# Delta stage of a hybrid encoder: the second and third sweep of the block solve on the open corner only

## Chip, cores and metric

One NeuronCore of one Trainium2 chip. The metric is the device time of the whole kernel in microseconds, as the median of a set of runs.

## The reference, cut to what matters

Two encoder layers over 2048 tokens of width 1024, in float32. Each layer projects its input, feeds one part to a gated DeltaNet branch (4 heads of width 128, run forward and backward over the sequence) and another to an attention branch, and maps both back. A final norm closes the trunk. The change lies in the DeltaNet branch, which for one direction is this, per chunk of tokens:

```python
lower = where(strict, einsum('bnhid,bnhjd->bnhij', k_beta, kc) * decay, 0.0)
a_mat = lower + eye(C)
rhs = concatenate([vc * bc, k_beta * exp(gc)[..., None]], axis=-1)
sol = triangular_solve(a_mat, rhs, left_side=True, lower=True, unit_diagonal=True)
u, w = sol[..., :Dv], sol[..., Dv:]
attn = einsum('bnhid,bnhjd->bnhij', qc, kc) * decay

def step(state, inp):                       # scan over the chunks
    v_new = u_i - w_i @ state
    o_i = (q_i * exp(g_i)[..., None]) @ state + a_i @ v_new
    state = state * exp(g_last)[..., None] + k_dec.T @ v_new
```

What has to be computed per chunk is thus the inverse of a unit triangular matrix, applied to the values, and a state that is carried from chunk to chunk.

## The kernel before, in words

The kernel is a sequence of stages per layer: input projection, token tables, `delta_net`, attention, output projection; and `finish` once. Each stage is one block in which the five engines run programs of their own, in a fixed order written by hand, and meet through semaphores. Only `delta_net` is touched.

**Tiling.** Its chunks are 128 tokens, not 64, so there are `NC` = 16 of them. "Side" 0 walks them forward, side 1 backward, so a step handles two chunks, and in each the 4 heads. A tile of one side is 128 partitions x 4 heads x 128 columns, one bank of PSUM wide. `each(out, left, right)` (L1146) issues the 4 matmuls of a tile, one per head; every one of them is recorded at line 1148, and shows as two records in the trace, since it is a float32 matmul.

**The inverse.** The 128x128 triangular matrix of a chunk is cut into 4x4 blocks of `BLK` = 32. The inverses of the 32x32 diagonal blocks come from a lane-wise elimination (`eliminate`, L1382 on GpSimd, L1465 on VectorE), in 5 groups of chunks, many blocks at once. `prepare_lanes` and `scale_lanes` on VectorE (L1478, L1486) bring a group in and out; the results go through DRAM and come back as block-diagonal tiles `dd` and `dt` (`load_dd`, `load_dt`). The rest of the inverse comes from a block substitution: `off_diagonal` (TensorE, L1184) and `masked_blocks` (VectorE, L1502) make `btc`, the strictly block-triangular factor; then three sweeps, each `y = dd - btc.T @ y` with `y = dd` at first: `substitute` (TensorE, L1190) and `update` (VectorE, L1507). Sweep k makes the blocks right that lie k off the diagonal. All three sweeps work on the whole 128x128 tile.

**The order.** The item of step j+1 (its inverse) is made during step j, between the pieces of the recurrence. TensorE's order in a step, each for both sides: `known`, `carried`, `off_diagonal`, `solve`, `turn_k`, from step 9 `turn_output`, `substitute` 1, `output`, `substitute` 2, `state_step`, `substitute` 3. The item of step 0 is made ahead of the loop, the last step makes none. VectorE's order in a step: from step 9 `mean_squares`; `remainder`, from step 9 `inverse_root`, `masked_blocks`, from step 9 `gate`, `update` 1, `visit`, `update` 2, `new_state`, `update` 3; then in steps 1 and 4 `prepare_lanes(3)` and `(4)`, in steps 2, 5 and 7 `scale_lanes(2)`, `(3)` and `(4)`. `scale_lanes(g)` waits for all of the elimination of group g.

GpSimd eliminates group 1 ahead of the loop and then has, in steps 0 to 7, a share of the columns of groups 2 to 4 (`SCAN_COLS`), each followed by `masked_scores` of the next step (L1394), which `output` of that step needs. From step 8 on it joins the two visits of a chunk, squares them and multiplies by the inverse mean instead. ScalarE scales what comes out of PSUM. SyncE issues all loads and stores of the stage in one order; `load_dd(j + 2)` waits for the third `update` of both sides of item j+1.

Of the kernel before, what the change touches and what calls it, by code (L numbers as in the profile page):

```python
# [7 lines left out]
P = 128  # L8
F32 = mybir.dt.float32
F32R = mybir.dt.float32r  # L10
ALU = mybir.AluOpType
# [23 lines left out]
BLK = 32  # L35
# [839 lines left out]
HEADS = range(DN_HEADS)  # L875
# [67 lines left out]
def delta_net(nc, a, c, l):  # L943
# [6 lines left out]
    with ExitStack() as stack, semaphores(nc, names) as s:  # L950
# [8 lines left out]
        dd, dt = (c.sq_acc[:, n * SEQ // 2:(n + 1) * SEQ // 2].rearrange("p (n h t) -> p n h t", n=N_DIR, t=P)  # L959
                  for n in range(2))  # L960
# [6 lines left out]
        r, se, oa, sq, ot, z, o, first_o, btc, y, am, kk = (room[:, n] for n in range(12))  # L967
# [6 lines left out]
        bank = lambda n: ps[:, n, :].rearrange("p (h t) -> p h t", h=DN_HEADS)  # L974
        mask = lambda side, kind: masks[:, side, kind, :].unsqueeze(1).broadcast_to([P, DN_HEADS, P])
        heads = lambda side: range(side * DN_HEADS, (side + 1) * DN_HEADS)
        inverse, chain, outer, turned = (lambda side: bank(side)), (lambda side: bank(2 + side)), \
            (lambda side: bank(4 + side)), (lambda side: bank(6 + side))

        with nc.Block() as block:  # L980
# [164 lines left out]
            def _(pe):  # L1145
                def each(out, left, right):  # L1146
                    for h in HEADS:
                        mm = nc.tensor.matmul(out[:, h, :], left[:, h, :], right[:, h, :], start=True, stop=True)  # L1148
                    return mm
# [40 lines left out]
                def substitute(side, i, k):  # L1190
                    if k == 1:
                        pe.wait_ge(s["dd_loaded"], 64 * (i + 1))
                        pe.wait_ge(s[f"btc{side}"], i + 1)
                        each(inverse(side), btc[:, side], dd[:, side]).then_inc(s[f"p{side}"], 1)
                    else:
                        pe.wait_ge(s[f"y{side}"], 3 * i + k - 1)
                        each(inverse(side), btc[:, side], y[:, side]).then_inc(s[f"p{side}"], 1)

                def known(side, j):
                    pe.wait_ge(s[f"state{side}"], j + 1)  # L1200
# [44 lines left out]
                for k in (1, 2, 3):  # L1245
                    for side in SIDES:
                        substitute(side, 0, k)
                for j in range(NC):
                    more = j + 1 < NC
                    for side in SIDES:  # L1250
                        known(side, j)
                    for side in SIDES:
                        carried(side, j)
                    for side in SIDES:
                        if more:
                            off_diagonal(side, j + 1)
                    for side in SIDES:
                        solve(side, j)
                    for side in SIDES:
                        if more:  # L1260
                            turn_k(side, j + 1)
                    if j > FIRST_VISITS:
                        for side in SIDES:
                            turn_output(side, j - 1)
                    for side in SIDES:
                        if more:
                            substitute(side, j + 1, 1)
                    for side in SIDES:
                        output(side, j)
                    for side in SIDES:  # L1270
                        if more:
                            substitute(side, j + 1, 2)
                    for side in SIDES:
                        state_step(side, j)
                    for side in SIDES:
                        if more:
                            substitute(side, j + 1, 3)
# [177 lines left out]
            def _(dve):  # L1455
# [51 lines left out]
                def update(side, i, k):  # L1507
                    dve.wait_ge(s[f"p{side}"], 3 * i + k)
                    if k == 1:
                        dve.wait_ge(s["dd_loaded"], 64 * (i + 1))  # L1510
                        if i:
                            dve.wait_ge(s[f"solve{side}"], i)
                    nc.vector.tensor_tensor(y[:, side], dd[:, side], inverse(side), ALU.subtract).then_inc(s[f"y{side}"], 1)

                def visit(side, j):
                    dve.wait_ge(s[f"out{side}"], j + 1)
# [53 lines left out]
                for k in (1, 2, 3):  # L1570
                    for side in SIDES:
                        update(side, 0, k)
                    if k == 1:
                        prepare_lanes(2)
                scale_lanes(1)
                for j in range(NC):
# [14 lines left out]
                    if more:  # L1591
                        for side in SIDES:
                            update(side, j + 1, 1)
                    for side in SIDES:
                        visit(side, j)
                    if more:
                        for side in SIDES:
                            update(side, j + 1, 2)
# [605 lines left out]
def build(nc, a):  # L2204
# [6 lines left out]
    with ExitStack() as stack:  # L2211
# [23 lines left out]
        for l in range(DEPTH):  # L2235
            input_projection(nc, a, c, l)
            token_inputs(nc, a, c, l)
            delta_net(nc, a, c, l)
            with ExitStack() as inner:
                c.delta = inner.enter_context(nc.sbuf_tensor(f"ahead_delta{l}", [P, DN_HEADS, SEQ], F32))  # L2240
                c.gates = inner.enter_context(nc.sbuf_tensor(f"ahead_gates{l}", [P, DN_HEADS, SEQ], F32R))
                c.w_out = inner.enter_context(nc.sbuf_tensor(f"ahead_w{l}", [P, 2, KT * P], F32))
                attention(nc, a, c, l)
                output_projection(nc, a, c, l)
# [72 lines left out]
```

## Time and profile before

| | |
|---|---|
| runs | 4149.61, 4154.29, 4154.32 us; median 4154.29 |
| profiled execution | 4156.78 us, its span 4155.0 us |
| TensorE (PE) | 3827.0 us busy, 92% of the span |
| VectorE (DVE) | 2846.4 us, 69% |
| ScalarE (ACT) | 1874.4 us, 45% |
| GpSimd (POOL) | 715.7 us, 17% |
| granted TensorE clock, mean | 0.955 |

The busy shares are averages over stages that differ much. GpSimd's 17%, for instance, lies nearly all in two places of each layer. PEld is TensorE's weight load, which overlaps its matmuls; SPq is the queue of SyncE, at which DMAs are issued. In the rows, "x16" is the number of merged instructions, and for TensorE 128*64 would be a weight tile of 128 rows and 64 columns. A bracket at the end of a timeline row is the engine's idle time before it and who ended it. The dn_banks are PSUM; the dn_sb_room tile holds `y`, `btc`, `r`, `am` and eight more, c_sq_acc holds `dd` and `dt`. Matmul ends are modelled and pipelined, so the time between two starts says more than a duration.

### The profile page before, as it was taken

What the parts mean: (1) busy time and instruction counts of PE and PEld (TensorE: products, weight loads), DVE (VectorE), ACT (ScalarE), POOL (GpSimd) and SP (SyncE); (2) the same over time, 40 slices, a digit from 0 to 9 for tenths busy, and PEclk for the clock granted to TensorE, in tenths of its full rate; (3) what the DMA queues carried; (4) which work ended last, traced back from release to release, by engine and by line L of the source; (5) the groups of instructions that cost most, each with busy time, mean ns of one, the idle gap of its engine ahead of it and who ended that gap; (6) DMA issues with size and microseconds to landing.
All of it is one profiled execution on the core that took longest, in us unless ns stands there. A gap on an engine that the chain in (4) does not pass through costs nothing. (4 is left out here: it accounts for less than half of the span.)

```text
span 4155.0 us, 55812 instructions
## 1 busy us (share of the span) xinstructions
PE 3827.0 (92%) x19078; PEld 3004.4 (72%) x19078; DVE 2846.4 (69%) x3424; ACT 1874.4 (45%) x2552; POOL 715.7 (17%) x761
## 2 busy tenths in 40 slices
PE   7999996699799999999999999966997999999896
PEld 5877785599766776767778777845996767776674
DVE  5674182676689999975266723745776999999743
ACT  4222212255377777772132222133554777777511
POOL 0022102596400000000001211037942000000000
PEclk9999998899899999999999999978998999999997
DMA  2111174445530000005322113654454200000335
GB/s 117 72 66 73 64 257 133 125 135 153 142 121 22 25 24 22 25 13 176 144 103 77 62 72 128 221 148 117 136 153 128 93 26 24 22 25 20 90 145 227
DMA packets 335765, 407.71 MB, mean 98 GB/s; under 512 B 105872, under 2 KB 255504, under 8 KB 315224
## 3 DMA queue, kind: packets, MB, share of 16 engines
q1 hardware_dynamic: 332728, 384.67, 28.9%
q10 hardware_dynamic: 2880, 20.97, 1.2%
q8 instruction: 95, 1.56, 0.2%
q14 instruction: 62, 0.51, 0.0%
HBM read 265.70 MB, written 139.66 MB: 98 GB/s over the span
## 5 line engine op out<-in xcount | busy, mean ns | idle before, releaser
L1854 DVE TENSOR_REDUCE att_sb_part<-att_banks 128x1 f32<-128x512 f32 x992 | 680.4, 687 | 102.7 <-PE att_banks L1739 88.8
L1841 ACT ACTIVATE att_sb_probs<-att_banks 128x1024 f32<-128x1024 f32 x512 | 525.1, 1026 | 314.0 <-PE att_banks L1767 313.8
L1872 DVE TENSOR_TENSOR att_sb_p_lo<-att_sb_probs,att_sb_p_hi 128x1024 fp32r<-128x1024 f32 x512 | 622.8, 1216 | 22.3 <-ACT att_sb_p_hi L1845 22.2
L1845 ACT ACTIVATE att_sb_p_hi<-att_sb_probs 128x1024 fp32r<-128x1024 f32 x512 | 544.1, 1063 | 16.1
L341 PE MATMUL proj_banks<-proj_sb_h_hi,proj_sb_w_hi 128*128 128x512 f32 x1600 | 500.9, 394 | 9.8 <-DVE proj_sb_pad L535 9.8
L341 PE MATMUL proj_banks<-proj_sb_h_lo,proj_sb_w_hi 128*128 128x512 f32 x1600 | 498.7, 393 | 0.0
L341 PE MATMUL proj_banks<-proj_sb_h_hi,proj_sb_w_low 128*128 128x512 f32 x1600 | 497.6, 392 | 0.0
L1148 PE MATMUL dn_banks<-dn_sb_room 128*128 128x128 f32 x3072 | 379.6, 283 | 58.0 <-DMA dn_sb_room<-proj 21.3
L401 POOL TENSOR_TENSOR c_low_squares<-c_sq_acc,proj_sb_high_squares 128x2048 fp32r<-128x2048 f32 x28 | 141.0, 5037 | 1679.8 <-ACT c_sq_acc L462 1679.8
L1148 PEld LDWEIGHTS dn_banks<-dn_sb_room 128*128 128x128 f32 x3072 | 368.0, 198 | 80.6 <-DMA dn_sb_room<-proj 30.9
L1766 PE MATMUL att_banks<-att_sb_q,att_sb_k 128*128 128x512 f32 x1024 | 407.0, 397 | 3.2 <-DVE att_sb_q L1866 1.9
L1767 PE MATMUL att_banks<-att_sb_q,att_sb_k 68*128 68x512 f32 x1024 | 409.1, 400 | 0.0
L1784 PE MATMUL att_banks<-att_sb_p_hi,att_sb_v_hi 128*65 128x512 f32 x1024 | 403.1, 394 | 1.4 <-DVE att_sb_p_lo L1872 1.4
L1739 PE MATMUL att_banks<-att_sb_k,att_sb_q 128*128 128x512 f32 x992 | 399.4, 404 | 3.9 <-DVE att_sb_part L1854 3.9
L1784 PE MATMUL att_banks<-att_sb_p_lo,att_sb_v_hi 128*65 128x512 f32 x1024 | 402.8, 393 | 0.0
L1784 PE MATMUL att_banks<-att_sb_p_hi,att_sb_v_lo 128*65 128x512 f32 x1024 | 400.8, 391 | 0.0
L341 PEld LDWEIGHTS proj_banks<-proj_sb_h_hi,proj_sb_w_hi 128*128 128x128 f32 x1600 | 301.4, 189 | 84.7 <-issue 11.0
L341 PEld LDWEIGHTS proj_banks<-proj_sb_h_lo,proj_sb_w_hi 128*128 128x128 f32 x1600 | 301.0, 188 | 75.6
L341 PEld LDWEIGHTS proj_banks<-proj_sb_h_hi,proj_sb_w_low 128*128 128x128 f32 x1600 | 300.8, 188 | 72.4
L617 DVE SCALAR_TENSOR_TENSOR proj_sb_out<-proj_sb_pad,proj_sb_taps,proj_sb_out 128x2048 f32<-128x2048 f32 x96 | 276.6, 2882 | 3.4
L535 DVE TENSOR_TENSOR proj_sb_out<-proj_banks,proj_sb_scale 128x1024 f32<-128x1024 f32 x56 | 68.5, 1223 | 272.7 <-PE proj_banks L341 272.7
L1739 PEld LDWEIGHTS att_banks<-att_sb_k,att_sb_q 128*128 128x128 f32 x992 | 189.7, 191 | 80.0 <-DVE att_sb_part L1854 7.9
(233 smaller groups left out, 5412.0 us busy)
## 6 DMA issues: line engine op xcount, KB each, us to landing
proj<-proj_sb_out SPq DMA_DIRECT2D x40, 1024.0 KB, 3.9
dn_sb_kq<-proj SPq DMA_DIRECT2D x64, 512.0 KB, 4.7
proj_sb_w_raw<-in_w_in SPq DMA_DIRECT2D x52, 536.0 KB, 3.6
dn_sb_room<-proj SPq DMA_DIRECT2D x32, 768.0 KB, 5.1
att_sb_q<-att_q SPq DMA_DIRECT2D x64, 256.0 KB, 2.6
x_res<-ahead_delta SPq DMA_DIRECT2D x16, 1024.0 KB, 4.1
proj_sb_pad<-proj SPq DMA_DIRECT2D x24, 512.0 KB, 4.7
proj<-proj_sb_out ACTq DMA_DIRECT2D x12, 1024.0 KB, 4.3
```

Source lines behind the costliest of these rows:

```text
L341: mm = nc.tensor.matmul(ps[:, 2 * half + n, :], w[:, u, k, :], h[:, k, at:at + QB], start=(k == 0 and w is w_hi and h is h_hi), stop=(k == ...
L401: nc.gpsimd.tensor_tensor(low, raw, high[:].bitcast(F32), ALU.subtract).then_inc(s["squares_split"], 1)
L617: nc.vector.scalar_tensor_tensor(out=out[:, u, :], in0=src, scalar=taps[:, u, j:j + 1], in1=out[:, u, :], op0=ALU.mult, op1=ALU.add).then_ ...
L1148: mm = nc.tensor.matmul(out[:, h, :], left[:, h, :], right[:, h, :], start=True, stop=True)
L1739: nc.tensor.matmul(ps[:, 4 + u % 2, :], q1[:, slot, tile * P:(tile + 1) * P], k1[:, slot % 2, keys * QB:(keys + 1) * QB], start=True, stop ...
L1766: nc.tensor.matmul(out, k1[:, slot % 2, keys], q1[:, slot, :], start=True, stop=False)
L1767: mm = nc.tensor.matmul(out, k2[:, slot % 2, keys], q2[:, slot, :], start=False, stop=True)
L1784: mm = nc.tensor.matmul(ps[0:DH + 1, 6 + kv, :], part_v[:, kv, tile, 0:DH + 1], part_p[:, at, m, :], start=opens, stop=(tile == NC - 1 and ...
L1841: nc.scalar.activation(probs[:, pair % 2], ps[:, 2 * (pair % 2):2 * (pair % 2) + 2, :], ACT.Exp, scale=SCALE).then_inc(s["exp_done"], 1)
L1845: nc.scalar.activation(p_hi[:, pair % SLOTS], probs[:, pair % 2], ACT.Copy).then_inc(s["hi_done"], 1)
L1854: nc.vector.tensor_reduce(part[:, w // NQ, w % NQ:w % NQ + 1], ps[:, 4 + w % 2, :], AX.X, ALU.max) \
L1872: nc.vector.tensor_tensor(p_lo[:, pair % SLOTS], probs[:, pair % 2], p_hi[:, pair % SLOTS].bitcast(F32), ALU.subtract).then_inc(s["lo_done ...
```

## The change

`open_rows` and `open_cols` name the corner of a side that is still open in sweep k: for side 0 the first 128 - 32 k rows and the last 128 - 32 k columns, for side 1 the mirror of it. In the second and the third sweep both engines work on that corner alone, 64x64 and 32x32: the matmul takes those weight columns of `btc` (they are the rows of the result) and those columns of `y`, with all 128 partitions in the sum as before, and the subtraction takes those rows and columns. The first sweep, the waits, the order and the numbers of instructions stay.

```diff
+        open_rows = lambda side, k: slice(0, P - k * BLK) if side == 0 else slice(k * BLK, P)
+        open_cols = lambda side, k: slice(k * BLK, P) if side == 0 else slice(0, P - k * BLK)
@@ substitute (TensorE), k = 2, 3
                         pe.wait_ge(s[f"y{side}"], 3 * i + k - 1)
-                        each(inverse(side), btc[:, side], y[:, side]).then_inc(s[f"p{side}"], 1)
+                        rows, cols = open_rows(side, k), open_cols(side, k)
+                        for h in HEADS:
+                            mm = nc.tensor.matmul(inverse(side)[rows, h, cols], btc[:, side, h, rows], y[:, side, h, cols],
+                                                  start=True, stop=True)
+                        mm.then_inc(s[f"p{side}"], 1)
@@ update (VectorE)
-                    nc.vector.tensor_tensor(y[:, side], dd[:, side], inverse(side), ALU.subtract).then_inc(s[f"y{side}"], 1)
+                        nc.vector.tensor_tensor(y[:, side], dd[:, side], inverse(side), ALU.subtract).then_inc(s[f"y{side}"], 1)
+                    else:
+                        rows, cols = open_rows(side, k), open_cols(side, k)
+                        nc.vector.tensor_tensor(y[rows, side, :, cols], dd[rows, side, :, cols], inverse(side)[rows, :, cols],
+                                                ALU.subtract).then_inc(s[f"y{side}"], 1)
```

## Rows read from the trace of the kernel before

**Rows 1.** Stretches: bounds, length; busy PE, PEld, DVE, ACT, POOL; clock, DMA.

```profile
825.00:970.00 145.00, 139.34 (x1219) 138.13 (x1218) 101.45 (x170) 76.52 (x259) 130.63 (x208) 0.99 0.46 133
...
976.40:981.00 4.60, 4.60 (x21) 4.60 (x22) 2.16 (x6) 2.12 (x9) 0.00 (x0) 0.50 0.20 48
...
981.00:1108.00 127.00, 126.59 (x1127) 125.81 (x1126) 93.43 (x189) 64.66 (x234) 64.03 (x57) 1.00 0.53 145
```

**Rows 2.** Timeline of a late step: start, us, engine, line, count, idle before; last row a group.

```profile
1001.23 7.31 PE L1148 MATMUL dn_banks<-dn_sb_room 128*128 128x128 f32 x64
...
1004.11 0.69 DVE L1513 TENSOR_TENSOR dn_sb_room<-c_sq_acc,dn_banks 128x512 f32<-128x512 f32 x1 [0.20 <-PE dn_banks L1148]
...
1006.79 0.69 DVE L1527 TENSOR_TENSOR dn_sb_state<-dn_sb_room,dn_banks 128x512 f32<-128x512 f32 x1 [0.21 <-PE dn_banks L1148]
...
1008.38 3.74 PE L1148 MATMUL dn_banks<-dn_sb_state,dn_sb_kq 128*128 128x128 f32 x32
...
1009.18 0.68 DVE L1534 TENSOR_REDUCE dn_sb_mean<-dn_sb_room 128x4 f32<-128x512 f32 x1
1009.33 1.80 SPq L1054 DMA_DIRECT2D c_sq_acc<-d_blk  x4
...
1010.87 2.15 DVE L1497 SCALAR_TENSOR_TENSOR dn_sb_room<-dn_banks,c_tok,dn_sb_vv 128x128 f32<-128x128 f32 x8
...
1013.74 1.95 PE L1148 MATMUL dn_banks<-dn_sb_room 128*128 128x128 f32 x16
...
1017.27 1.95 PE L1148 MATMUL dn_banks<-c_sq_acc,dn_sb_room 128*128 128x128 f32 x16
...
1019.05 7.31 PE L1148 MATMUL dn_banks<-dn_sb_room 128*128 128x128 f32 x64
...
L1148 PE MATMUL dn_banks<-dn_sb_room 128*128 128x128 f32 x3072 | 379.6, 283 | 58.0 <-DMA dn_sb_room<-proj 21.3 <-DVE dn_sb_room L1513 19.4 <-DVE dn_sb_room L1497 17.1
```

**Rows 3.** Timeline around the seam between steps 7 and 8; last, the second layer.

```profile
952.99 2.50 POOL L1397 TENSOR_TENSOR dn_sb_room<-dn_sb_att,dn_sb_masks 128x512 f32<-128x512 f32 x2
...
959.07 7.31 PE L1148 MATMUL dn_banks<-dn_sb_room 128*128 128x128 f32 x64
...
969.82 0.25 POOL L1392 TENSOR_TENSOR dn_sb_lane_inv<-dn_sb_lane_inv,dn_sb_lane_tmp 128x31 f32<-128x31 f32 x1
...
970.11 2.89 DVE L1488 TENSOR_TENSOR dn_sb_lane_mat<-dn_sb_lane_inv,dn_sb_lane_beta 64x1024 f32<-64x1024 f32 x1 [3.00 <-POOL dn_sb_lane_inv L1392]
...
976.38 3.78 PE L1148 MATMUL dn_banks<-dn_sb_room 128*128 128x128 f32 x16 [4.64 <-DVE dn_sb_room L1497]
...
3014.72 2.88 DVE L1488 TENSOR_TENSOR dn_sb_lane_mat<-dn_sb_lane_inv,dn_sb_lane_beta 64x1024 f32<-64x1024 f32 x1 [3.02 <-POOL dn_sb_lane_inv L1392]
```

**Rows 4.** Groups of weight loads by form: after the bar busy us and mean ns.

```profile
L1148 PEld LDWEIGHTS dn_banks<-dn_sb_room 128*128 128x128 f32 x3072 | 368.0, 198 | 80.6 <-DMA dn_sb_room<-proj 30.9 <-DVE dn_sb_room L1513 19.8 <-DVE dn_sb_room L1497 19.2
...
L1784 PEld LDWEIGHTS att_banks<-att_sb_p_hi,att_sb_v_hi 128*65 128x65 f32 x1024 | 140.8, 138 | 75.0 <-DVE att_sb_p_lo L1872 2.8 <-issue 0.4
...
L352 PEld LDWEIGHTS proj_banks<-c_low_squares,proj_sb_w_hi 128*32 128x32 f32 x112 | 12.1, 108 | 4.8
```

**Rows 5.** Timeline of TensorE in the input projection, with and without 128*32.

```profile
204.88 0.61 PE L341 MATMUL proj_banks<-proj_sb_h_hi,proj_sb_w_low 128*128 128x512 f32 x2
205.33 0.40 PE L352 MATMUL proj_banks<-proj_sb_high_squares,proj_sb_w_hi 128*32 128x512 f32 x1
205.57 0.62 PE L341 MATMUL proj_banks<-proj_sb_h_hi,proj_sb_w_hi 128*128 128x512 f32 x2
...
216.00 0.63 PE L341 MATMUL proj_banks<-proj_sb_h_lo,proj_sb_w_hi 128*128 128x512 f32 x2
216.47 0.63 PE L341 MATMUL proj_banks<-proj_sb_h_hi,proj_sb_w_low 128*128 128x512 f32 x2
```

**Rows 6.** Timeline of VectorE in the token tables: smaller operations out of PSUM.

```profile
673.88 0.42 DVE L809 TENSOR_TENSOR tab_sb_x<-tab_banks,tab_sb_low 128x256 f32<-128x256 f32 x1
...
675.09 0.29 DVE L818 COPY tab_sb_token_sums<-tab_banks 128x128 f32<-128x128 f32 x1
```

## The prediction

> **What bounds the kernel now.** I read the view of stretches first, cut at the seam that the timeline shows inside the delta stage of the first layer [rows 1]. From 825 to 970 us (steps j = 0 to 7) TensorE is busy 139.3 of 145 us, but GpSimd is busy 130.6 of 145 as well, in 208 instructions, and the list of waits has none of GpSimd's there: the rest of its time is the small gap behind each instruction of its dependent chain. From 981 to 1108 us (steps 8 to 15) TensorE has 126.6 of 127 us at the full clock and GpSimd only 64. So there are two regimes.
>
> The timeline of a late step [rows 2] shows what TensorE's line looks like: output, sweep 2, state and sweep 3 of both sides are one run of 64 records (two records to a matmul, eight matmuls for each of the four) from 1001.23 to the next group at 1008.38, which is 7.15/64 = 0.112 us from record to record. The same group starts again at 1019.05: a step is 17.82 us, with no gap in it.
>
> The seam [rows 3] is where the two regimes meet. GpSimd's last elimination instruction for lane group 4 ends at 970.07; only then can VectorE start `scale_lanes(4)`, for which it has waited 3.00 us; the `remainder` of step 8 stands behind it on VectorE, and TensorE, which needs that for `solve`, idles 4.64 us and starts at 976.38. The second layer has the same wait, 3.02 us at 3014.72. Since GpSimd waited for nobody on the way, the time of the seam is GpSimd's and not TensorE's.
>
> **The change, part by part.** *Fewer columns, TensorE.* Per item the second and the third sweep have 2 sides x 4 heads = 8 matmuls each, so 16 records each. At 0.112 us that is 1.79 us per sweep, 3.57 us per item. A record of the second sweep now loads 64 instead of 128 weight columns and streams 64 instead of 128; of the third, 32 and 32.
>
> No row shows such a record, so I bound the record-to-record time from both sides. The low end is proportional: 0.056 and 0.028 us. What speaks for it: a weight load's own duration falls with its columns, 198 ns at 128, 138 at 65, 108 at 32, about 0.9 ns a column over a constant near 80 ns that overlaps [rows 4]. The high end is 0.112 us, unchanged: the 128-column pace is the shortest that rows 2 to 6 have, and nothing in them shows that instructions can follow more closely. As the loads do shrink, I stay nearer to the low end, with some room for a fixed part: 0.062 us for the second and 0.045 us for the third. Gain per item: 16 x (0.112 - 0.062) + 16 x (0.112 - 0.045) = 0.80 + 1.07 = 1.87 us. Behind each sweep the first full load (state, then `known`) has only a short matmul to hide under instead of a long one: 0.05 us twice, taken off. Left are 1.77 us per item; proportional scaling would give 2.24 us, the unchanged pace 0.
>
> *Switching the array's shape.* The matmuls with 64 and 32 output rows stand between full ones. The nearest rows are in the input projection [rows 5]: two 128*128 matmuls, then one 128*32, then 128*128 again. The pair takes 0.45 us, the 128*32 one 0.24 us, three in 0.69; two neighbours without any switch take 0.47 us. So a switch costs less than 0.01 us there; I take 0. The upper bound is the full latency of a record being waited out, mean 0.283 against a pace of 0.112 [rows 2, 4]: 0.17 us per switch, four switches a step, 0.68 us. The Trainium skill, "TensorEngine Tiling (Array Packing)", section Key Properties, says that changing the tiling mode, as against the tile, drains TensorE; by that rule the sum would lose those 0.68 us a step and the kernel come out near 4139 us. Rows 5, where such a change happens twice in every three matmuls, don't show it.
>
> *VectorE.* Its two subtractions per side shrink from 128x512 (0.69 us) to 64x256 and 32x128. The nearest rows are a 128x256 subtraction at 0.42 us and a 128x128 copy at 0.29 us [rows 6]. That takes (0.27 + 0.40) x 2 = 1.3 us a step off an engine that isn't the bound; by itself worth nothing, and at worst (fixed costs, no shrinking) 0.
>
> *What is late next in steps 8 to 14.* In the times of rows 2, with sweep 2 at 0.5 us a side and sweep 3 at 0.36: output ends 1003.0, sweep 2 at 1004.0, state at 1005.8 (0.89 a side), sweep 3 at 1006.5; `known` starts there instead of at 1008.38. It needs the new state: VectorE starts 0.20 us behind the end of a side's state matmuls and takes 0.69 us [rows 2], so 1005.8 for side 0 (0.7 us to spare) and 1006.7 for side 1, needed at 1007.4. Sweep 3 needs the second update, which can't start before VectorE has done both visits (1003.9) and ends by 1004.8; it is needed at 1005.8. Further on, `remainder` started 2.5 us behind `known` (1010.87 against 1008.38) because two mean squares stood in front of it, from 1009.18; they now start 0.1 us sooner relative to `known`, so `solve` finds it with the same 0.7 us to spare (8 pieces from 1010.87 for 2.15 us, `solve` at 1013.74). The last update frees `dd` for SyncE's four loads, at 1009.33 before; issued by 1011.1, needed at 1017.27. No wait is added, and SyncE's order stays. So in these seven steps the whole 1.77 us comes through.
>
> *Steps 0 to 7 and the first item.* They get the same 1.77 us each, and none of it reaches the end. VectorE reaches `scale_lanes(4)` up to 14 us earlier and waits there until 970.1 as before. Already on the way TensorE meets GpSimd: `output` of step 7 starts at 959.07, and its masked scores come off GpSimd at 952.99 + 2.50 = 955.49 [rows 3], so from there only 3.6 us of lead fit. The sweeps of item 0 lie ahead of `scale_lanes(1)`, which waits for GpSimd too. Longer idling may lower TensorE's clock; it is at 0.50, the 1.2 GHz level, from 976.4 to 981.0 already [rows 1], behind the 4.64 us of idling, so I count no change.
>
> *Sum.* 7 steps x 1.77 us x 2 layers = 24.8 us. The profiled execution took 4156.8 us (span 4155.0): 4132.0. The median of the runs is 4154.3, 2.5 us lower, inside their spread of 4149.6 to 4154.3; taken from it the forecast is 4129.5, call it 4130 us.
>
> **Rivals.**
> *A: small matmuls have a large fixed cost*, by a drain at each switch or a floor near 0.08 us. By the floor: 32 x 0.032 x 14 = 14 us, 4140; by the drain: (1.77 - 0.68) x 14 = 15 us, 4139; both together: 4149. For it: no row has records closer than 0.112 us. Against it: rows 4 and 5.
> *B: GpSimd isn't a wall*, and all 32 items save: 4154 - 32 x 1.77 = 4098 us. For it: TensorE is 96% busy in steps 0 to 7. Against it: the waits of 3.00 and 3.02 us at the seam, equal in both layers.
> *C: the pace doesn't fall at all*, because instructions can't be issued faster: only VectorE's work shrinks, and that is covered. 4154 us.
> *D, slower:* the pace stays at 0.112 us and every switch drains. 0.68 us a step: 4.8 us in steps 8 to 14, and in steps 0 to 7 5.4 us, of which the seam absorbs 3.0. 7.2 us per layer, 4169 us. It decides once the four switches cost more than the records save, so from a fixed 0.44 us a switch at my pace, or from zero at an unchanged one. Rows 5 speak against it.
> That the change doesn't do what it says can be left out: sweep k only alters blocks k or more off the diagonal, and those are the rows and columns kept.
>
> **How the numbers follow.** Forecast 0.70 (its own range 4122 to 4137), A 0.13, B 0.07, C 0.05, D 0.05. A difference under 0.2%, 8.3 us, can't be told from no change. Faster by more than that (below 4146): the forecast, B and two thirds of A, 0.86. Within it: the rest of A and nearly all of C, 0.09. Slower: D, 0.05. The proportional end gives 14 x 2.24 = 31 us, 4123, and with the 2 or 3 us by which the medians of two sets differ 4120; that is the low end, with B left out. The high end takes in A but for its worst mixture: 4146.
>
> **What would show it.** In the stretch of steps 8 to 15 the distance from one `known` group to the next should fall from 17.82 to about 16.05 us, TensorE still without gaps; sweep 2 and 3 should stand as groups of about 1.0 and 0.7 us for 16 records. In steps 0 to 7 the step at the seam should still start its `solve` near 976.4 counted from the same start of the loop, with VectorE's wait for L1392 grown from 3.0 us to 5 or more. VectorE's subtractions should read about 0.42 and 0.29 us. I am wrong if the seam moves, if gaps on TensorE show up in steps 8 to 14, or if 16 small records take over 1.3 us.

## The result: 20 us, and where they lie

The changed kernel takes 4134.6 us in the median (4126.46 to 4140.22, five runs), the one before 4153.97 (4149.61 to 4154.32): a ratio of 0.995 (0.9937 to 0.9964). 4130 was forecast, 4120 to 4146 the range. The profiled execution is the slowest of the five, 4140.22 us with a span of 4138.4 and a mean clock of 0.951.

First the late step again, as [rows 2] have it. The columns are start, us, engine, line, count, idle before. Lines have moved by two to ten; L1201 is the new matmul of sweeps 2 and 3, L1522 its subtraction.

```profile
1007.56 3.84 PE L1150 MATMUL dn_banks<-dn_sb_state,dn_sb_kq 128*128 128x128 f32 x32
...
1009.10 0.86 DVE L1546 SCALAR_TENSOR_TENSOR dn_sb_mean<-dn_sb_mean,c_q_eps 128x4 f32<-128x4 f32 x1
...
1011.23 2.16 DVE L1503 SCALAR_TENSOR_TENSOR dn_sb_room<-dn_banks,c_tok,dn_sb_vv 128x128 f32<-128x128 f32 x8
1011.24 1.95 PE L1150 MATMUL dn_banks<-c_sq_acc,dn_sb_w 128*128 128x128 f32 x16
...
1018.34 1.95 PE L1150 MATMUL dn_banks<-dn_sb_room 128*128 128x128 f32 x16
1020.22 0.97 PE L1201 MATMUL dn_banks<-dn_sb_room 128*64 128x64 f32 x16
...
1020.94 0.87 DVE L1522 TENSOR_TENSOR dn_sb_room<-c_sq_acc,dn_banks 64x256 f32<-64x256 f32 x2
...
1021.12 2.05 PE L1150 MATMUL dn_banks<-dn_sb_room 128*128 128x128 f32 x16
1023.10 0.59 PE L1201 MATMUL dn_banks<-dn_sb_room 128*32 128x32 f32 x16
1023.62 3.84 PE L1150 MATMUL dn_banks<-dn_sb_state,dn_sb_kq 128*128 128x128 f32 x32
...
1023.81 0.59 DVE L1522 TENSOR_TENSOR dn_sb_room<-c_sq_acc,dn_banks 32x128 f32<-32x128 f32 x2
```

From `known` to `known` the step takes 1023.62 - 1007.56 = 16.06 us, against 17.82 before, still without a gap. Read by starts, sweep 2 takes 0.90 us (0.056 a record) and sweep 3 takes 0.52 us (0.033 a record). The full groups around them have grown: output takes 1.88 us and state 1.98, where a full group of 16 without a neighbour of another form takes 1.79. `known`, 3.57 us before, takes 3.68 (1007.56 to 1011.24). VectorE's subtractions come in pairs of 0.87 and 0.59 us, so about 0.44 and 0.30 each, close to the 0.42 and 0.29 that were put down.

Next the seam, and how the loop starts and ends. Its last three rows are of the second layer.

```profile
833.80 3.57 PE L1150 MATMUL dn_banks<-dn_sb_room 128*128 128x128 f32 x16 [4.18 <-DVE dn_sb_room L1503]
...
957.71 2.38 PE L1150 MATMUL dn_banks<-dn_sb_room 128*128 128x128 f32 x16 [1.52 <-POOL dn_sb_room L1403]
...
973.50 2.87 DVE L1494 TENSOR_TENSOR dn_sb_lane_mat<-dn_sb_lane_inv,dn_sb_lane_beta 64x1024 f32<-64x1024 f32 x1 [9.29 <-POOL dn_sb_lane_inv L1398]
...
979.75 3.78 PE L1150 MATMUL dn_banks<-dn_sb_room 128*128 128x128 f32 x16 [10.70 <-DVE dn_sb_room L1503]
...
1092.71 2.19 PE L1150 MATMUL dn_banks<-dn_sb_room 128*128 128x128 f32 x16 [1.01 <-DVE dn_sb_room L1503]
...
1105.63 2.11 PE L1230 MATMUL dn_banks<-c_ident,dn_sb_room 128*128 128x128 f32 x8 [5.15 <-POOL dn_sb_room L1421]
...
2867.14 3.78 PE L1150 MATMUL dn_banks<-dn_sb_room 128*128 128x128 f32 x16 [5.00 <-DVE dn_sb_room L1503]
...
3012.79 3.78 PE L1150 MATMUL dn_banks<-dn_sb_room 128*128 128x128 f32 x16 [9.88 <-DVE dn_sb_room L1503]
...
3139.29 2.12 PE L1230 MATMUL dn_banks<-c_ident,dn_sb_room 128*128 128x128 f32 x8 [5.14 <-POOL dn_sb_room L1421]
```

VectorE's wait for GpSimd has grown from 3.00 to 9.29 us and TensorE's gap from 4.64 to 10.70. Counted from `solve` of step 0, step 8 starts its `solve` after 145.95 us; before it was 145.39 (976.38 less 830.99 in the profile before). So eight narrower steps buy nothing. The stretches say the same, in the columns of [rows 1]:

```profile
833.00:979.75 146.75, 126.28 (x1216) 121.28 (x1217) 91.35 (x174) 76.96 (x264) 130.29 (x205) 0.97 0.48 139
979.75:984.40 4.65, 4.65 (x24) 4.65 (x25) 2.17 (x6) 2.18 (x9) 0.00 (x0) 0.57 0.20 48
```

GpSimd's 130.3 us are those of [rows 1]; TensorE is down to 126 of 147. Behind the gap the granted clock averages 0.57 of full over 4.65 us, against 0.50 before; in the second layer it averages 0.50 in both kernels (3012.79 to 3017.44, and 3020.98 to 3025.63 before). The longer idling has not made that stretch slower.

A measure that the rest uses is the **length of the loop**: from `solve` of step 0 to the last turn, the one that waits 5.15 us for GpSimd. In the profile before these are the rows

```profile
830.99 3.46 PE L1148 MATMUL dn_banks<-dn_sb_room 128*128 128x128 f32 x16 [4.13 <-DVE dn_sb_room L1497]
...
1114.09 2.11 PE L1224 MATMUL dn_banks<-c_ident,dn_sb_room 128*128 128x128 f32 x8 [5.16 <-POOL dn_sb_room L1415]
```

Before it is 283.10 us in the first layer and 283.14 in the second; changed it is 271.83 and 272.15, so 11.3 and 11.0 us less. The forecast was 7 x 1.77 = 12.4 for each.

### The profile page after: what moved, and what is told of

It is laid out like the page before. It is cut to its first block and busy times, and to the rows that moved or that the text cites. A ratio compares the mean times of both kernels' runs of the same rounds, so it can differ in the third digit from the quotient of the medians.

```text
span 4138.4 us, 55812 instructions
## 1 busy us (share of the span) xinstructions
PE 3777.8 (91%) x19078; PEld 2942.7 (71%) x19078; DVE 2813.9 (68%) x3424; ACT 1872.0 (45%) x2552; POOL 716.5 (17%) x761
## 5 line engine op out<-in xcount | busy, mean ns | idle before, releaser
L1150 PE MATMUL dn_banks<-dn_sb_room 128*128 128x128 f32 x2048 | 268.2, 286 | 63.3 <-DVE dn_sb_room L1503 34.0
L1150 PEld LDWEIGHTS dn_banks<-dn_sb_room 128*128 128x128 f32 x2048 | 251.6, 199 | 88.1 <-DMA dn_sb_room<-proj 36.8
L535 DVE TENSOR_TENSOR proj_sb_out<-proj_banks,proj_sb_scale 128x1024 f32<-128x1024 f32 x56 | 68.4, 1222 | 272.1 <-PE proj_banks L341 272.1
```

## Experiments

**Both regimes apart: only the late items narrow, only the early ones.** `e1_again` is the changed kernel once more, on the chip of the two others.

```diff
-                        rows, cols = open_rows(side, k), open_cols(side, k)
+                        rows, cols = (open_rows(side, k), open_cols(side, k)) if i > FIRST_VISITS else (slice(0, P), slice(0, P))
 # on both engines; FIRST_VISITS = 8. e3_early_only has "i <= FIRST_VISITS"
```

> The changed kernel once more, nothing altered. Its runs lay 14 us apart (4126 to 4140), those of before 5 us, and the profiled one was the slowest: it gained 16.6 us against the profiled one before, not 24.8. Theory: the seven late steps of each layer gain 12.3 us in every execution (a step of 16.06 us), and what differs between executions lies ahead of the loop of the delta stage, where the waits for the chunks' loads differ; this profile again shows 16.06 us a step, the median is 4126 to 4140. Rival: the changed step itself varies from run to run; then the step in this profile isn't 16.06.

> The narrow sweeps only for items 9 to 15, which are made in steps 8 to 14; items 0 to 8 full. Theory (GpSimd's elimination is a wall for steps 0 to 7): all of the gain is here, 14 x 1.77 = 24.8 us at most, time as the changed kernel within 3 us. Rival B (no wall): 14 of 32 items, so 14/32 of what all give; with 20 us for all it would be 9 us.

> The narrow sweeps only for items 0 to 8, made ahead of the loop and in steps 0 to 7; items 9 to 15 full. Theory: no gain, 4154 within 4 us, VectorE's wait for GpSimd at the seam (scale_lanes(4)) 9 us instead of 3.0, the step after it 17.82 us. Rival B: 18 of 32 items, 11 us or more of the 20.

Measured, as ratios to the kernel before: all items 0.9938 (0.9921 to 0.9956), late only 0.9948 (0.993 to 0.9966), early only 1.0005 (0.9993 to 1.0017). The loops take 272.1 and 270.8 us, 271.9 and 272.0, 283.0 and 284.1. The late step of `e1_again` is again 16.06 us (1004.27 to 1020.33), as expected. VectorE's row at the seam, late only and then early only:

```profile
973.97 2.88 DVE L1494 TENSOR_TENSOR dn_sb_lane_mat<-dn_sb_lane_inv,dn_sb_lane_beta 64x1024 f32<-64x1024 f32 x1 [3.02 <-POOL dn_sb_lane_inv L1398]
```

```profile
972.87 2.87 DVE L1494 TENSOR_TENSOR dn_sb_lane_mat<-dn_sb_lane_inv,dn_sb_lane_beta 64x1024 f32<-64x1024 f32 x1 [7.82 <-POOL dn_sb_lane_inv L1398]
```

The late items, 14 of 32, carry all of it as far as the spread of the runs lets one see: the two intervals overlap, and so do the loops. What the early items save turns into a longer wait in front of that one row (7.82 us, where 9 were expected), and rival B is gone.

**VectorE alone narrow.** TensorE's matmuls are full again, the subtractions stay narrow.

```diff
 substitute (TensorE)
-                        rows, cols = open_rows(side, k), open_cols(side, k)
+                        rows, cols = slice(0, P), slice(0, P)
```

> TensorE's sweeps full again, VectorE's second and third subtraction on the corner only. Theory: VectorE isn't the bound, 0 us, 4154 within 4 us, the late step 17.82 us. Rival: VectorE's shorter work lets remainder or the state start sooner and carries part of the gain, then 5 us or more.

Ratio 1.0005 (0.9995 to 1.0015), loops 283.4 and 283.6 us, a late step of 17.83 (1011.27 to 1029.10): the shorter subtractions are worth nothing, as was put down for them. TensorE's gap at the seam is 7.13 and 6.27 us there, against 4.64 and 4.65: what they free in the early steps ends at the wall.

**Which width sets the pace: weights or stream.** Each ran once.

```diff
 substitute (TensorE)
-                        rows, cols = open_rows(side, k), open_cols(side, k)
+                        rows, cols = open_rows(side, k), slice(0, P)     # e5_weights_only
+                        rows, cols = slice(0, P), open_cols(side, k)     # e6_stream_only
```

> Second and third sweep: 64 and 32 weight columns, but all 128 columns streamed; VectorE as in the change. Theory: a record takes as long as the longer of its load and its stream, so the pace stays at 0.112 us and only the cost of switching the array's shape shows: the late step is 17.82 plus what four switches cost, which the trace of the changed kernel puts at 0.1 us each, so 18.2. Rival: loads are what sets the pace; then the step falls below 17.8.

> Second and third sweep: all 128 weight columns loaded, 64 and 32 columns streamed; no switch of the array's shape. Theory: the load of 128 columns sets the pace at 0.112 us or a little less, step 17.8 or 17.5, no extra time at the seams between groups. Rival: the stream sets the pace; then the step falls to 16 us or less, and to less than the 16.06 us of the changed kernel, since no switch is paid.

The kernels took 4153.99 and 4156.64 us, the one before 4154.64 beside them; one execution each says nothing at this spread, so the reading rests on the rows. TensorE's timeline, `e5_weights_only` first, with narrow weights and full stream:

```profile
1009.00 3.84 PE L1150 MATMUL dn_banks<-dn_sb_state,dn_sb_kq 128*128 128x128 f32 x32
...
1019.79 1.95 PE L1150 MATMUL dn_banks<-dn_sb_room 128*128 128x128 f32 x16
1021.67 1.58 PE L1201 MATMUL dn_banks<-dn_sb_room 128*64 128x128 f32 x16
1023.18 2.05 PE L1150 MATMUL dn_banks<-dn_sb_room 128*128 128x128 f32 x16
1025.16 1.53 PE L1201 MATMUL dn_banks<-dn_sb_room 128*32 128x128 f32 x16
1026.62 3.84 PE L1150 MATMUL dn_banks<-dn_sb_state,dn_sb_kq 128*128 128x128 f32 x32
```

```profile
1005.00 1.95 PE L1150 MATMUL dn_banks<-dn_sb_room 128*128 128x128 f32 x16
1006.79 1.90 PE L1201 MATMUL dn_banks<-dn_sb_room 128*128 128x64 f32 x16
1008.52 2.00 PE L1150 MATMUL dn_banks<-dn_sb_room 128*128 128x128 f32 x16
1010.36 1.87 PE L1201 MATMUL dn_banks<-dn_sb_room 128*128 128x32 f32 x16
1012.07 3.82 PE L1150 MATMUL dn_banks<-dn_sb_state,dn_sb_kq 128*128 128x128 f32 x32
1015.72 1.95 PE L1150 MATMUL dn_banks<-c_sq_acc,dn_sb_w 128*128 128x128 f32 x16
...
1029.90 3.82 PE L1150 MATMUL dn_banks<-dn_sb_state,dn_sb_kq 128*128 128x128 f32 x32
```

Starts apart, over 16 records, in us a record (64 at 64 and 32 at 32 from the changed kernel):

| weight columns | 128 streamed | 64 | 32 |
|---|---|---|---|
| 128 | 0.112 | 0.108 | 0.107 |
| 64 | 0.094 | 0.056 | |
| 32 | 0.091 | | 0.033 |

A load of 128 columns holds the pace near 0.107 whatever is streamed behind it, and a stream of 128 holds it near 0.091 however short the load. Only both together bring it far down, and then nearly in proportion. For `e5_weights_only` a step of 18.2 us was expected, the pace unchanged and the switches on top; it was 17.62 (1009.00 to 1026.62), a miss of the pace. On the switches this run speaks clearly: its full groups take 1.88 and 1.98 us, exactly those of the changed kernel, while with full weights and a narrow stream the group ahead stays at 1.79 (1005.00 to 1006.79). So the 0.1 us in front of a narrow group belongs to the change of the weight tile's form. Behind one, the narrow stream costs something by itself too: in `e6_stream_only` state takes 1.84 us and `known` 3.65, 0.05 and 0.08 more than without. That run had been expected to show no extra time there; these 0.13 us are why its step stays at 17.83 (1012.07 to 1029.90) although its sweeps are 0.14 us shorter.

**Each sweep by itself.** Third sweep on 64x64 like the second; and second sweep full, third narrow.

```diff
-                        rows, cols = open_rows(side, k), open_cols(side, k)
+                        rows, cols = open_rows(side, 2), open_cols(side, 2)                              # e10_both_64
+                        rows, cols = (open_rows(side, k), open_cols(side, k)) if k == 3 else (slice(0, P), slice(0, P))  # e11_third_only
```

> The third sweep on the same 64x64 corner as the second. Theory: record pace follows the size, 0.056 instead of 0.033 us, the four switches stay at 0.1 us: late step 16.06 + 16 x 0.023 = 16.44 us. Rival: the switch cost depends on how small the tile is or on there being two small sizes; then less.

> Second sweep full, third on the 32x32 corner. Theory: two switches instead of four, each 0.1 us, and the third sweep's 0.52 instead of 1.79 us: 17.82 - 1.27 + 0.2 = 16.75 us a late step.

TensorE at the end of the step, `e10_both_64` and then `e11_third_only`:

```profile
1008.33 3.84 PE L1150 MATMUL dn_banks<-dn_sb_state,dn_sb_kq 128*128 128x128 f32 x32
...
1023.87 0.97 PE L1201 MATMUL dn_banks<-dn_sb_room 128*64 128x64 f32 x16
1024.76 1.49 PE L1150 MATMUL dn_banks<-dn_sb_state,dn_sb_kq 128*128 128x128 f32 x11
```

```profile
1008.21 3.84 PE L1150 MATMUL dn_banks<-dn_sb_state,dn_sb_kq 128*128 128x128 f32 x32
...
1020.78 1.95 PE L1201 MATMUL dn_banks<-dn_sb_room 128*128 128x128 f32 x16
1022.56 1.95 PE L1150 MATMUL dn_banks<-dn_sb_room 128*128 128x128 f32 x16
1024.44 0.59 PE L1201 MATMUL dn_banks<-dn_sb_room 128*32 128x32 f32 x16
1024.96 1.27 PE L1150 MATMUL dn_banks<-dn_sb_state,dn_sb_kq 128*128 128x128 f32 x9
```

The kernels took 4141.6 and 4143.29 us, one execution each; their steps are 16.43 and 16.75 us, both as the table and 0.1 us a switch add them up. In the second kernel a full sweep 2 stands ahead of the state group, and that group takes 1.88 (one switch, at its end) instead of 1.98 (two). The loops take 273.8 and 274.9 us, 275.9 and 276.4; seven steps of 1.39 and 1.07 us saved off 283.1 would be 273.4 and 275.6.

**Moving the wall.** Lane group 4 feeds items 14 and 15 only, so its elimination need not end in step 7. `e7_wall_moved` is the changed kernel with GpSimd's columns of group 4 spread over steps 5 to 10; `e8_wall_moved_full` is the same on the kernel before.

```diff
-SCAN_COLS: 5: [(3, 4), (4, 6)], 6: [(4, 12)], 7: [(4, 13)]
+SCAN_COLS: 5: [(3, 4), (4, 6)], 6: [(4, 8)], 7: [(4, 8)], 8: [(4, 4)], 9: [(4, 3)], 10: [(4, 2)]
-SCALED = {2: 2, 5: 3, 7: 4}
-STORED = {3: 2, 6: 3, 8: 4}
+SCALED = {2: 2, 5: 3, 10: 4}
+STORED = {3: 2, 6: 3, 11: 4}
```

> The changed kernel, and the elimination of lane group 4, which is only needed by item 14, is spread: 8 columns each in steps 6 and 7, then 4, 3 and 2 in steps 8 to 10, scaled at the end of step 10 instead of 7, stored in step 11. Theory (the wall is what swallows the gain of steps 0 to 7): the solve of step 8 comes 10 to 13 us earlier in each layer; the late scaling costs 2 to 4 us of that. 4130 minus 14 to 22: 4108 to 4118. Rival: something else (VectorE's order, the loads of d_blk) holds steps 0 to 7 to the same pace; then under 5 us.

> The same spreading in the kernel before, with full sweeps. Theory: TensorE needs 16.95 us a step in steps 0 to 7, so only what it idles at the seam comes back, 4.6 us and the low clock behind it, less the late scaling: 0 to 5 us per layer, 4144 to 4154. Rival: the spreading itself is what gives the gain, as large as in the kernel with narrow sweeps.

4112.64 us (4107.87 to 4118.01), ratio 0.9903 (0.9887 to 0.9918), and for the full sweeps 4142.55 us (4136.67 to 4146.54), 0.9972 (0.9961 to 0.9983), somewhat faster than expected. TensorE of `e7_wall_moved` where the seam was, its new wait, and the end of its loop:

```profile
835.11 3.78 PE L1150 MATMUL dn_banks<-dn_sb_room 128*128 128x128 f32 x16 [5.77 <-DVE dn_sb_room L1503]
...
970.46 1.95 PE L1150 MATMUL dn_banks<-dn_sb_room 128*128 128x128 f32 x16
...
1020.52 3.43 PE L1150 MATMUL dn_banks<-dn_sb_room 128*128 128x128 f32 x16 [2.58 <-DVE dn_sb_room L1503]
...
1098.54 2.11 PE L1230 MATMUL dn_banks<-c_ident,dn_sb_room 128*128 128x128 f32 x8 [5.16 <-POOL dn_sb_room L1421]
```

Step 8's `solve` follows without a gap, 135.35 us behind that of step 0 instead of 145.95. `scale_lanes(4)` still costs 2.58 us in step 11, since `remainder` stands behind it on VectorE; the loads of `dd` and `dt` cost 5.1 us in three waits. The loops take 263.4 and 259.5 us. With the wall where it was the narrow sweeps are worth 4153.97 - 4134.6 = 19.4 us; with the wall moved, 4142.55 - 4112.64 = 29.9. This version beats both kernels.

**Hiding `scale_lanes` in a gap of VectorE.** `e9_into_gap` is `e7_wall_moved` with the lane work moved from the end of a step to behind `masked_blocks`, where VectorE waits for TensorE anyway. Each `scale_lanes` thus moves from the end of one step into the next (SCALED 2, 5, 10 become 3, 6, 11), while TensorE's `turn_lanes` stays in steps 2, 5 and 10.

```diff
+                    if j in PREPARED:            # behind masked_blocks, before gate and update 1
+                        prepare_lanes(PREPARED[j])
+                    if j in SCALED:
+                        scale_lanes(SCALED[j])
...
-                    if j in PREPARED: ...        # was the end of the step
+PREPARED = {1: 3, 5: 4}; LANES_IN = {0: 3, 4: 4}; SCALED = {3: 2, 6: 3, 11: 4}; STORED = {3: 2, 7: 3, 12: 4}
```

> The kernel with the wall moved, and VectorE's lane work (prepare_lanes and scale_lanes, 3.5 to 5 us) moved from the end of a step, where remainder and so TensorE's solve stand behind it, into the step, behind masked_blocks, where VectorE waits 2 to 3 us for TensorE in any case. Theory: the idle time and the low clock that TensorE still shows at the steps with lane work (0.9 to 1.2 us in two early steps, 2.6 us and 1.6 us of low clock in step 11 of the profile before this one) go, 4 to 6 us per layer: 4100 to 4105. Rival: the lane work now delays gate and update 1, and sweep 2 waits for those; no gain.

A miss: 4124.56 us (4118.33 to 4127.02), 0.9934 (0.9921 to 0.9948), 12 us slower than without the move. Its loops are 265.4 and 268.3 us long, 1.9 and 8.8 more. The waits of TensorE in the second layer's loop, `e7_wall_moved` and then `e9_into_gap` (total, times, longest):

```profile
PE dn_banks L1150 <- DVE dn_sb_room L1503: 9.6, 5, 5.2
...
PE dn_banks L1150 <- DMA c_sq_acc<-d_blk: 3.9, 3, 2.0
```

```profile
PE dn_banks L1150 <- DMA c_sq_acc<-d_blk: 12.8, 5, 6.5
...
PE dn_banks L1150 <- DVE dn_sb_room L1503: 5.9, 2, 4.9
```

The wait for `remainder` went down by 3.7 us, as meant, and the one for the loads of `dd` and `dt` up by 8.9; waits for GpSimd are up by 1.1. Most of the rest of the 8.8 us in that loop is clock: TensorE is busy 247.9 us at a granted mean of 0.96, in `e7_wall_moved` 245.4 at 0.98. The first layer has a wait for the loads as long as the longest of these, 6.53 us; here it is with SyncE's queue ahead of it, and last the same loads in `e7_wall_moved`:

```profile
887.53 1.10 SPq L1036 DMA_DIRECT2D d_blk<-dn_sb_lane_mat  x2
...
891.09 1.29 SPq L1040 DMA_DIRECT2D d_blk<-dn_sb_lane_raw  x1
892.49 4.13 SPq L1056 DMA_DIRECT2D c_sq_acc<-d_blk  x4
...
903.33 3.78 PE L1150 MATMUL dn_banks<-c_sq_acc,dn_sb_w 128*128 128x128 f32 x16 [6.53 <-DMA c_sq_acc<-d_blk]
```

```profile
892.04 4.15 SPq L1056 DMA_DIRECT2D c_sq_acc<-d_blk  x4
```

SyncE issues in one order. The stores of a lane group wait for `scale_lanes`, and the loads of the blocks stand behind the stores. Counted from `solve` of step 0, those loads are issued at 61.1 us (892.49 less 831.43), in `e7_wall_moved` at 56.9 (892.04 less 835.11): 4.1 us later, while TensorE is free for them 1.6 us sooner. The timelines show this order; a version that also stores a step later, which would test it, was not run.

## Why the prediction was right, and where two errors cancelled

- **"7 steps x 1.77 us x 2 layers".** Mechanism and size hold, the size partly by luck (next two points): 1.76 us a step in the late steps, and late-only gives the whole gain. 11.3 and 11.0 us a loop came of 12.4.
- **The pace, 0.062 and 0.045 us.** Too careful. It was 0.056 and 0.033, the proportional end for sweep 2 and nearly so for sweep 3. The gain of the sweeps alone is 3.57 - 0.90 - 0.52 = 2.15 us a step, not 1.87.
- **"A switch costs less than 0.01 us there; I take 0."** This step failed. With the form of the weights changing between small matmuls a switch costs 0.10 us, four in a step: output + 0.09, state + 0.19, `known` + 0.11 (3.68 from its start to `carried`, 3.57 before), together 0.39 us. Against it stood 0.10 us for two short covers, which `e6_stream_only` measures by themselves at 0.13 us. 2.15 - 0.39 = 1.76, so the pace (0.28 us too little gain) and the switches (0.29 us too little cost) cancel to 0.01 us by luck. [Rows 5] were the wrong place to read it: their matmuls stream 512 columns, and no cost shows between those. The Trainium skill, "TensorEngine Tiling (Array Packing)", section Key Properties, has a change of mode drain TensorE; the trace agrees that there is a price with the weight tile's form, and puts it at 0.10 us, below the 0.17 that waiting out a whole record was reckoned at.
- **"`solve` finds it with the same 0.7 us to spare".** Failed in the last step. `remainder` starts 3.67 us behind `known` (1011.23 against 1007.56) instead of 2.49: the small operation of the two mean squares takes 0.86 and 0.60 us, where it took 0.26 and 0.17 before. In the first layer of both profiles it takes 0.16 or 0.17 us where GpSimd is idle, and 0.26 to 0.87 where GpSimd is at work; with the sweeps shorter both of them fall into GpSimd's masked scores (1008.67 to 1011.17). That GpSimd is what holds it up is likely, but no run isolates it. In steps 8 to 14 there is just enough left, as the 16.06 us without a gap show; in step 15, which makes no next item, `solve` waits 1.01 us. That is most of what both loops fall short of 12.3 by (1.0 and 1.3 us).
- **"None of it reaches the end", steps 0 to 7.** Held. `e3_early_only` gives nothing; VectorE's wait grew to 9.29 us ("5 or more"). Not foreseen: TensorE now also waits in the early steps, for loads of `dd` and `dt` (5.0 us in the first layer, 0.7 before) and for masked scores (the 1.52 us at 957.71), which costs nothing as long as the wall stands. It costs some once the wall is moved. Step 8's `solve` moved by + 0.6 and + 0.2 us.
- **The clock.** Counted as unchanged behind the seam. It did not fall, but it isn't fixed either: from `solve` to the next `known` step 8 takes 11.75 us where the 4.65 us behind the gap average 0.57, and 12.38 where they average 0.50 (second layer). `e1_again`, the same kernel, has 12.43 us at 0.50 and 11.26 at 0.67. So the same loop can be up to 1.2 us shorter by the clock alone; this is why the first loop gained 11.3 us although its seam came 0.6 us late, and it goes most of the way to the 270.8 us in `e1_again`.
- **The rest up to the median.** The two loops save 22.3 us, the two profiled executions lie 16.6 apart and the medians 19.4. The difference lies outside the loop: waits for chunk loads before it (`dn_sb_room<-proj`) come to 21.3 us in the profile before, and to 26.7 and 24.1 in two executions of the same changed kernel. They are not all of it: `e1_again`, with 2.8 us more of them than before, is 2.1 us shorter outside its loops. Where `solve` of step 0 starts in the first layer is no mark of the sweeps either: 831.0, 834.8, 833.7 and 833.0 us in four kernels whose item 0 has full ones on TensorE (before, `e2_late_only`, `e4_vector_only`, `e8_wall_moved_full`), 830.3 and 833.8 in the two executions of the changed kernel. These waits stand ahead of the stage's first sweep. Whether anything but chance moves them stays open.

Of the rivals, A had part of the truth (a price for each switch) and the wrong sum. B fell by `e3_early_only`, C by the late step, D by the pace.

## What to carry to other kernels

Cut the plan at the place where two engines trade the lead, and count a saving only on the side where the engine that you speed up has it: here 14 of the 32 items were worth all of the 20 us and the other 18 nothing. Then ask whether the wall has to stand there; moving it was worth another 22 us and made the same edit worth 30. And when work is moved within an engine's order, follow the DMA queue that waits for it first: a gap in VectorE was filled, and the loads behind its stores came late.

## What the runs showed of the hardware that I had not expected

- The pace of small float32 matmuls stays near whichever is long, the load (0.107 us a record with 128 weight columns and 32 streamed) or the stream (0.091 with 32 and 128). With both short it falls on to 0.056 us at 64 by 64 and 0.033 at 32 by 32; no floor showed down to there.
- Narrow weights behind full ones, or the other way round, cost about 0.10 us a change when the matmuls are small, at a full stream of 128 as well (`e5_weights_only`). A full group behind a narrow stream with full weights is longer by 0.05 to 0.08 us (`e6_stream_only`).
- Narrowing one side alone is worth little: 0.20 us a step with narrow weights and a full stream, nothing with a narrow stream alone (17.83 us against 17.82).
- A VectorE operation on 128x4 elements took 0.16 or 0.17 us with GpSimd idle and up to 0.87 us beside GpSimd's 128x512 operations.
- The kernel before, run 23 times on one chip, lies between 4145.88 and 4167.27 us, a spread about as wide as the effect; medians of several runs, and the length of the loop inside the profile (270.8 to 272.2 us in the six loops with narrow late items, 283.0 to 284.1 in the six with full late sweeps of before, `e3_early_only` and `e4_vector_only`), were what could be read.
